# FF2 of a two-block transformer kernel: gate and up as seven block products, and a down phase of its own

## The reference

```python
h = rmsnorm(x, pre_ffn_w[l])
f = (jax.nn.silu(h @ w_gate[l]) * (h @ w_up[l])) @ w_down[l]
x = x + rmsnorm(f, post_ffn_w[l])
```

## Time and profile before

| | us |
|---|---|
| median of 3 runs | 2928.12 |
| lowest, highest run | 2925.88, 2928.41 |
| span of the profiled execution | 2927.6 |

### The profile page before, as it was taken

How to read it: one execution, slowest core, us unless ns; L and a number is a source line. 1 busy time by engine, 2 the same in 40 slices (tenths; PEclk the granted TensorE clock), 3 DMA queues, 4 the chain that set the end, 5 groups by cost and what they waited for, 6 DMA issues and landing times.

```text
span 2927.6 us, 31598 instructions
## 1 busy us (share of the span) xinstructions
PE 2866.2 (98%) x13123; PEld 2327.1 (79%) x13123; DVE 1388.7 (47%) x1658; ACT 961.0 (33%) x1266; POOL 368.1 (13%) x328
## 2 busy tenths in 40 slices
PE   9999999999999999999999999999999999999997
PEld 7877678888888888788878888666787888888886
DVE  6775544453535354543234444665655213233335
ACT  4313442321312121321236656654353221111112
POOL 1213112000000000111002222133321000000003
PEclk9999999999999999999999999999999999999999
DMA  3215523111111111244523331674641111111113
GB/s 117 87 72 140 151 60 108 51 40 55 44 56 40 54 37 61 69 148 159 195 80 101 99 101 59 181 226 146 228 139 69 37 58 40 56 38 62 37 61 126
DMA packets 88623, 270.01 MB, mean 92 GB/s; under 512 B 12568, under 2 KB 17304, under 8 KB 88480
## 3 DMA queue, kind: packets, MB, share of 16 engines
q1 hardware_dynamic: 73984, 221.61, 24.2%
q0 software_dynamic: 14496, 46.38, 4.6%
HBM read 215.35 MB, written 52.59 MB: 92 GB/s over the span
## 4 chain that ended last, share of the span: by engine, by line
PE 84%; DVE 7%; ACT 4%; issue 2%; POOL 1%; DMA 1%; SPq 0%; DVEq 0%; POOLq 0%; ACTq 0%
PE ps L213 83%; DVE cacc L184 1%; ACT PB L178 1%; PE ps L216 1%; POOL ga L181 1%; DVE PB L184 1%; DVE YA L181 1%; POOL YA L181 0%; DVE AL L184 0%; DMA raw<-in_w_win 0%; DMA RBc<-scr_inv 0%; DVE stk L181 0%; DVE sqacc L181 0%; ACT gt L178 0%; DVE cv L181 0%
## 5 line engine op out<-in xcount | busy, mean ns | idle before, releaser
L213 PE MATMUL ps<-AH,wh 128*128 128x512 f32 (+1 forms) x2216 | 880.7, 397 | 23.5 <-DVE T L181 5.7
L213 PE MATMUL ps<-AH,wl 128*128 128x512 f32 (+1 forms) x2216 | 865.7, 391 | 0.0
L213 PE MATMUL ps<-AL,wh 128*128 128x512 f32 (+1 forms) x2216 | 865.4, 391 | 0.0
L181 DVE TENSOR_TENSOR wl<-raw,wh 128x1024 fp32r<-128x1024 f32 (+2 forms) x226 | 268.7, 1189 | 808.5 <-ACT wh L178 808.1
L213 PEld LDWEIGHTS ps<-AH,wh 128*128 128x128 f32 (+1 forms) x2216 | 416.1, 188 | 122.8 <-issue 14.4
L178 ACT ACTIVATE wh<-raw 128x1024 fp32r<-128x1024 f32 (+2 forms) x273 | 251.5, 921 | 766.0 <-PE ps L213 759.3
L213 PEld LDWEIGHTS ps<-AH,wl 128*128 128x128 f32 (+1 forms) x2216 | 415.9, 188 | 90.3
L213 PEld LDWEIGHTS ps<-AL,wh 128*128 128x128 f32 (+1 forms) x2216 | 416.5, 188 | 87.8 <-issue 2.9
L213 PE MATMUL ps<-UH,wh 128*128 128x512 f32 (+1 forms) x840 | 325.2, 387 | 0.0
L213 PE MATMUL ps<-UH,wl 128*128 128x512 f32 (+1 forms) x840 | 325.1, 387 | 0.0
L213 PE MATMUL ps<-UL,wh 128*128 128x512 f32 (+1 forms) x840 | 325.1, 387 | 0.0
(11 more groups left out here) (229 smaller groups left out, 3243.5 us busy)
## 6 DMA issues: line engine op xcount, KB each, us to landing
raw<-in_w_up SPq DMA_DIRECT2D x44, 512.0 KB, 3.4
raw<-in_w_gu SPq DMA_DIRECT2D x44, 512.0 KB, 3.4
raw<-in_w_w2in SPq DMA_DIRECT2D x32, 512.0 KB, 4.3
raw<-in_w_down SPq DMA_DIRECT2D x48, 256.0 KB, 2.6
raw<-in_w_down SPq DMA_DIRECT2D x32, 320.0 KB, 2.8
xin<-in_xT SPq DMA_DIRECT2D x16, 512.0 KB, 8.9
stk<-scr_ka SPq DMA_DIRECT2D x32, 256.0 KB, 8.0
raw<-in_w_w2v SPq DMA_DIRECT2D x16, 512.0 KB, 3.5
```

Source lines behind the costliest of these rows:

```text
L181: return Issued(self, self.e.tensor_tensor(out, a, b, op))
L213: return Issued(self, self.e.matmul(out, l, r, start=start, stop=stop))
```

## The change

**Gate and up.** Blocks 0 to 2 (`PLAIN = 3`) are made as before. For the other 19 (`NQ`) the pair gate/up of a block is one 2x2 block product: weights 2 (gate, up) x 2 (channel tiles 0 to 3, 4 to 7), activations 2 (channel tiles 0 to 3, 4 to 7) x 2 (halves of the tokens). It is made by Strassen's form in Winograd's arrangement: seven products of 4 x 3 = 12 matmuls instead of eight. It needs four sums of activation blocks (T1 to T4, made once by VectorE from the float32 values in `YA`, in the four calls `sums(k)`, then split into `TH`/`TL`) and, per hidden block, four sums of weight blocks (`s_sums`, VectorE) before the split of all seven weight blocks (`high` on ACT, `s_lows` on DVE). The seven results go round the eight banks; VectorE combines them (`gate`, `shared`, `shared_end`, `gate_end`, `value`, `value_end`), after ScalarE has copied the first (`taken`).

**Down.** The gated block (`UU`) is written to a DRAM scratch `s_u` (`spill`). After all 22 blocks a down phase runs in four passes p of 22 steps, w = 0 to 87: passes 0 and 1 for the first half of the tokens, 2 and 3 for the second, each for four of the eight output tiles. One step reads a weight piece of 128x512 (`d_load`, `d_high`, `d_low`; nine buffers) and uses the gated block k = w mod 22 (`u_load`, `u_high`, `u_low`); it is 4 x 3 = 12 matmuls into four banks, and the 22 steps are summed in PSUM. Pass 3 stops after 14 steps (`HELD`); ACT copies that partial sum to SBUF, and the other 8 steps are done in two groups of 256 tokens.

```diff
+PLAIN = 3
+NQ = NFF - PLAIN
+DW = 9
+HELD = 14
...
+    PARTS = [("B11", 0), ("B21", 1), ("T2", 5), ("T1", 4), ("B22", 6), ("T3", 2), ("T4", 3)]
...
     def pe_ff2(self, q):
...
+        def part(n, i):
+            name, b = self.PARTS[i]
+            out = self.s_bank(n, i)
+            q.wait_ge(S.sl, 4 * n + {0: 1, 1: 1, 5: 2, 6: 2, 4: 3, 2: 4, 3: 4}[b])
+            h, l = self.s_high(n, b), self.s_low(n, b)
+            for k in range(4):
+                if name[0] == "T":
+                    q.wait_ge(S.tl3, k + 1)
...
+        for n in range(NQ):
+            for i in range(7):
...
+                elif i == 0:
+                    q.wait_ge(S.ev2, 7 * (n - 1))
+                elif i == 1:
+                    q.wait_ge(S.snp, n)
+                else:
+                    q.wait_ge(S.ev2, 7 * (n - 1) + (1, 2, 3, 4, 6)[i - 2] if n else 0)
+                part(n, i)
...
+        for w in range(88):
+            p, k = w // 22, w % 22
+            q.wait_ge(S.dwl, w + 1)
+            q.wait_ge(S.dul, 22 * (p // 2) + k + 1)
+            if k == 0:
+                q.wait_ge(S.fe, 4 * (p - 1))
+            if w == 66:
+                q.wait_ge(S.fmu, 8)
...
+            if p == 3 and k >= HELD:
+                continue
+            for n in range(4):
+                if w == 0:
+                    q.wait_ge(S.snp, NQ)
+                    q.wait_ge(S.ev2, 7 * NQ - 6 if n < 3 else 7 * NQ)
+                last = k == (HELD - 1 if p == 3 else 21)
+                t = down(w, self.d_bank(p, n), n, every, k == 0, last)
...
+        for g in (1, 2):
+            c = slice(0, 256) if g == 1 else slice(256, 512)
+            q.wait_ge(S.fe, 12 if g == 1 else 16)
+            for n in range(4):
+                for k in range(HELD, 22):
+                    t = down(66 + k, self.d_bank(g + 1, n)[:, c], n, c, k == HELD, k == 21)
...
     def act_ff2(self, q):
...
+        for k in range(2):
+            second(k)
         self.w_high(q, TILE["gu", ("u", 1)])
+        second(2)
+        up(TILE["gu", ("u", 0)], 0)
         self.norm_sqrt(q, 7, 4, 4)
         q.wait_ge(S.nrow, 7)
         q.act(self.RB[:, HALF[1]], self.bank(5), ACT.Copy).then_inc(S.nrb)
...
+        up(TILE["gu", ("u", 0)], 1)
+        sums_high(0)
+        second(3)
+        silu(0)
+        sums_high(1)
+        self.w_high(q, TILE["gu", ("g", 2)])
+        sums_high(2)
+        up_whole(1)
+        silu(1)
+        self.w_high(q, TILE["gu", ("u", 2)])
+        sums_high(3)
+        for b in (0, 5, 4, 2):
+            high(0, b)
...
     def dve_ff2(self, q):
...
+        def s_sums(n):
+            q.wait_ge((S.sg0, S.sg1)[n % 2], 16 * (n // 2 + 1))
+            q.wait_ge((S.su0, S.su1)[n % 2], 16 * (n // 2 + 1))
+            q.wait_ge(S.prd, 7 * (n - 1))
+            a11, a12, a21, a22, s1, s2, s4 = [self.s_raw(n, b) for b in range(7)]
+            q.tt(s1, a21, a22, ALU.add).then_inc(S.ss)
             q.wait_own()
+            q.tt(s2, s1, a11, ALU.subtract).then_inc(S.ss)
+            q.wait_own()
+            q.tt(s4, s2, a12, ALU.subtract).then_inc(S.ss)
+            q.tt(a21, a11, a21, ALU.subtract).then_inc(S.ss)
...
+            if more:
+                s_lows(n + 1, 3)
+            else:
+                for w in range(7):
+                    d_low(w)
+                    if w < 4:
+                        u_low(w)
+            value(n)
+        value_end(NQ - 1)
...
+        for w in range(88):
+            if w >= 7:
+                d_low(w)
...
+            for p in range(3):
+                if w == 22 * (p + 1) + 2:
+                    evacuate(p)
...
+            if 67 <= w < 71:
+                q.wait_ge(S.nrow, 8)
+                for n in (2 * (w - 67), 2 * (w - 67) + 1):
+                    q.wait_ge(S.sD, 8)
+                    q.stt(self.YD[:, n, HALF[0]], self.YD[:, n, HALF[0]], self.V("postff", n), self.bank(6), ALU.mult,
+                          ALU.mult).then_inc(S.fmu)
...
     def sp_ff2(self, q):
...
+        def up_load(n):
+            q.wait_ge(S.prd, 7 * (n - 1))
+            q.dma(self.SWR[n % 2][:, 2:4, :].rearrange("p a b -> p (a b)"),
+                  self.io["w_gu"][("u", PLAIN + n), :, :]).then_inc((S.su0, S.su1)[n % 2], 16)
...
+        q.wait_ge(S.tr3, 16)
...
+        gate_load(0)
+        up_load(0)
```

More of the change, by code:

```diff
@@ L76, in weight_tiles @@
     t += [("w2out", (half, n), 1024) for half in range(2) for n in range(NT)]
[L77 to L81, removed]
+    for i in range(PLAIN):
+        t += [("gu", ("g", i), 1024), ("gu", ("u", i), 1024)]
     return t
@@ L110, in gemm_events @@
             out += [(s, 0), (s, 1)]
-    return out + [(LAST8 + n, g) for g in range(3) for n in range(NT)]
+    return out
 EVENTS = gemm_events()
@@ L400, in __init__ @@
[L400 to L403, removed]
+        self.snap = [Area(nc, lo + at * 1024, lo + at * 1024 + 2048).get("snap", [P, 512]) for at in (4, 6, 112)]
+        self.GG = Area(nc, lo + 8 * 1024, lo + 12 * 1024).get("gg", [P, NTOK])
+        self.UU = Area(nc, lo + 12 * 1024, lo + 16 * 1024).get("uu", [P, NTOK])
@@ L405, in V @@
+        self.DWT, self.DWR = [], []
+        for at in (-24, -20, -16, -12, -8, -4, 76, 8, 12):
+            one = Area(nc, lo + at * 1024, lo + at * 1024 + 4096)
+            self.DWR.append(Area(nc, one.lo + 2048, one.hi).get("dwr", [P, 512])[:, :])
+            self.DWT.append(tuple(one.get("dwt", [P, 512], F32R)[:, :] for _ in range(2)))
     def V(self, name, i=0, p0=0, p1=P):
@@ new lines, in down, with stats @@
+        def down(w, out, n, c, first, last):
+            wh, wl = self.DWT[w % DW]
+            uh, ul = self.DU[w % 22]
+            ws = slice(n * P, n * P + P)
+            q.mm(out, wh[:, ws], uh[:, c], first, False)
+            q.mm(out, wh[:, ws], ul[:, c], False, False)
+            return q.mm(out, wl[:, ws], uh[:, c], False, last)
+        def stats(n, t0, t1, b):
+            for t in range(t0, t1):
+                i = q.mm(self.bank(b)[:, t - t0:t - t0 + 1], self.accD[:, t * P:t * P + P], self.ones[:, 0:1], True, True)
+            i.then_inc(S.nst)
@@ new lines, in dve_ff2 @@
+        self.w_low(q, TILE["gu", ("u", 1)])
+        gate_half(0)
+        self.norm_recip(q, 7, self.rc8[:, 4:8], 4)
+        gate_half(1)
+        sums(0)
+        sums(1)
+        gated(0)
+        self.w_low(q, TILE["gu", ("g", 2)])
+        sums_low(0)
+        sums_low(1)
+        sums(2)
+        gate_whole(1)
+        gated(1)
+        self.w_low(q, TILE["gu", ("u", 2)])
+        sums_low(2)
+        sums(3)
+        sums_low(3)
+        s_sums(0)
+        s_lows(0, 0, 1, 2, 3)
+        gate_whole(2)
@@ new lines, in scaled @@
+        def scaled(n):
+            c = slice(512, 768)
+            q.wait_ge(S.nrow, 9)
+            q.wait_ge(S.sD, 16)
+            q.stt(self.YD[:, n, c], self.YD[:, n, c], self.V("postff", n), self.bank(1)[:, 0:256], ALU.mult,
+                  ALU.mult).then_inc(S.fmu)
+        out(1, 4)
+        for n in range(5, 8):
+            out(1, n)
+            square(1, n - 1)
+        square(1, 7)
+        out(2, 4)
+        out(2, 5)
+        square(2, 4)
+        self.norm_recip(q, 9, self.last_col(1), 2)
@@ L3147, in dve_ff2 @@
+        out(2, 6)
+        square(2, 5)
+        for n in range(4):
+            scaled(n)
+        out(2, 7)
+        square(2, 6)
+        square(2, 7)
+        for n in range(4, 8):
+            scaled(n)
         self.norm_recip(q, 10, self.last_col(2), 2)
-        c = GROUPS[2]
-        scales = self.bank(6)[:, 0:256].unsqueeze(1).to_broadcast([P, 4, 256])
+        c = slice(768, 1024)
+        scales = self.bank(2)[:, 0:256].unsqueeze(1).to_broadcast([P, 4, 256])
         for n in (0, 4):
```

682 lines of the change are left out of this document (427 added, 255 removed), and 4 rows, old and new, of the table SHARED.

## The result

The changed kernel takes 2906.60 us (median of 4 runs, 2905.17 to 2908.76) against 2928.26 for the kernel before (4 runs): a ratio of 0.9928, 95% interval 0.9914 to 0.9943, 21.7 us less. The forecast was 2909.

What follows compares the result with a forecast made beforehand. TensorE, busy 98% of the span, was taken as the bound. Blocks ending at 2627.5 us, plus down steps, seams, statistics and the last 38.0 us, gave a 2908.3 us span, median 2908.8; forecast range 2901 to 2917, overall 2887 to 2923.

Steps and rivals of the forecast that it cites:

- Matmuls and blocks: 19 gate/up blocks: 228 fewer matmuls at 0.2266 us save 51.7 us; each block lasts 19.04 us, with no waits inside.
- Rival D: Inside the blocks: TensorE waits in each for weight low halves or a bank, 2936 to 3018 us; chance 0.07.
- the 4.8 us of cover: Inside each block: VectorE works 14.2 of 19.04 us, leaving 4.8 us spare.
- Way in: Entry to FF2: TensorE waits 3.9 us before gate 2 and 3.3 before block 3; 13.1 us with the clock.
- half clock: Behind TensorE waits of about 3 us or more: clock falls to 1.2 GHz, costing 2.9 us on top.
- First seam: Blocks to down, step 0: 3.2 us wait for the last block's value plus 2.0 for the clock, 5.2 us.
- Second seam: Step 66: TensorE waits 7.5 us for VectorE's scalings of the first half; 10.4 us with the clock.
- Third seam: Step 80: 4.8 us wait for weight pieces split behind ScalarE's copies of held banks; 7.7 us with the clock.
- Statistics and end: From the first 256-column matmul to the span's end: 42.0 us less 5.4 plus 1.4, so 38.0 us.
- The five places: TensorE idle before gate 2 (3.9), block 3 (3.3), in step 0 (3.2), before steps 66 (7.5) and 80 (4.8).
- Rival B: At the seams: they are cheaper or the clock holds, 2898 us, or 2893 with the entry wait halved; chance 0.18.
- C: Matmuls slower with other operands, or seams at their upper bounds: 2915 to 2924 us, 2929 with both; chance 0.17.

Runs made afterwards that it cites:

- e7: Changed kernel plus three extra 128x1024 VectorE instructions in each of the 19 blocks, behind the value: 2910.86 us.
- e8: Changed kernel plus six extra 128x1024 VectorE instructions in each of the 19 blocks, behind the value: 2958.92 us.
- e9: Changed kernel with gate 2's and up 2's weights split ahead of the activation sums, VectorE's sums run together and wide low halves last: 2897.82 us.
- e3: Changed kernel with seven of the last block's nine down-phase low halves on VectorE moved behind that block's value: 2904.25 us.
- e1: Changed kernel with VectorE's eight scalings of the first half put three weight pieces earlier, ahead of pass 2's results: 2899.37 us.
- e6: Changed kernel with 32 TensorE matmuls of 128x512, whose result nobody reads, ahead of the wait of step 66: 2901.74 us.
- e5: Changed kernel with the three re-orderings e1, e2 and e3 together: 2887.03 us.
- e10: Changed kernel with the edits of e5 and e9 together: 2874.72 us.
- e4: Changed kernel with only gate 2's weight split (ScalarE) and low half (VectorE) put ahead of the activation sums: 2907.17 us.
- e2: Changed kernel with ScalarE's copies of the four held banks put behind its last weight piece (87): 2903.74 us.

## Why the prediction was right

**Matmuls and blocks.** 51.7 us from 228 x 0.2266: the count is exact, the pitch too (19 us a block). VectorE was costed at 14.2 us per block; it takes 13.4. Rival D stays out: VectorE can take on 3.7 us more per block without a wait (e7) and 7.3 not (e8), and the 4.8 us of cover in the prediction, 5.6 by the rows, lie between.

**Way in, 13.1 us.** The waits are 3.87 and 4.10, for 3.9 and 3.3. Block 3's was longer since the load of up took 5.6 us for 5.0; the four sums took 2.8 as counted. ScalarE's 128x2048 took 1.92 for 1.9. The half clock cost 2.8 us behind gate 2 (24.33 us from the first to the last of 96 starts, for 95 x 0.2266 = 21.53) for 2.9, but only 1.65 behind block 3, again for 2.9. So a wait 0.8 us too small and a half clock 1.2 us too large nearly cancel. e9 took 11.4 away and left 1.1: 12.5.

**First seam, 5.2 us.** Wait 3.17 for 3.2; e3: 5.05 in all, so 1.9 for the clock. I had taken 2.0 for it, between nothing and 2.9, without a row; that it fits is luck.

**Second seam, 10.4 us.** Wait 7.70 for 7.5; e1: 10.8, e6: 2.8 of it the clock. GpSimd's part was 1.7 us by the changed kernel's rows. I had 9.0 us for the seam if each low half waited for a full GpSimd instruction of 1.38 us. The two low halves began 0.43 and 0.15 us into one of 1.26 us, waited for its end and lost 0.7 and 1.0 us. The rule of the Trainium skill (SBUF — State Buffer, "Who interferes with whom"), that the two exclude each other, agrees with these rows; what failed was my working from it, which is its upper bound. The earlier trace rows already show the same: the instruction of 1.78 us ended at 2195.81, 0.54 us behind the GpSimd one beside it.

**Third seam, 7.7 us.** Wait 5.14 for 4.8 (the prediction's terms add to 4.7). The clock behind it costs 28.41 - 26.59 = 1.8 us (256-column matmuls up to the last statistics, changed kernel against e5), for 2.9: 6.9.

**Statistics and end.** I had 38.0 us from the first 256-column matmul to the end, with the clock counted at the seam; e5, where the clock stays up behind step 80, has 2887.2 - 2849.19 = 38.0. One reading was wrong and did no harm: the prediction calls the 1.56 us wait TensorE's only late one, but the trace before has others in the statistics, the longest 2.03 us ahead of the last sums at 2917.14.

**The step that was mis-sized** is the constant 2.9 us of half clock, taken from one wait. It was 2.8 at its largest and 1.4 at its smallest behind one and the same wait of 7.7 us, 1.65 behind block 3 and 1.8 at step 80. The five places come to 12.5 + 5.1 + 10.8 + 6.9 = 35.3 us in place of 36.4.

**The sum.** FF2 is 19.9 us shorter, for 2927.6 - 2908.3 = 19.3 forecast. The span missed by more (2902.9 for 2908.3), and 4.8 us of that lie ahead of the wait for `AL`, in code that didn't change: 2207.58 against 2202.74. The median, 2906.6 for 2908.8, fits better than the span, and that is luck: the prediction put the median 0.5 us above the span, as it had been for the kernel before, but here the profiled run was the fastest of the four, its own time 2905.17 lies 2.3 above its span, and the median lies 3.7 above. Rival B's 2898 and C's bounds did not come. B's figure for all seams gone was 2872.7, 55.4 us less; e10's median is 2874.7. By FF2 time it is 50.7 us less, and its waits of 1.11 and 1.89 us and the 1.45 us of half clock behind the second are 4.5 of the 4.7 that are missing.

## What to carry to other kernels

When a bound engine gets less work, add up its waits at the entry, the seams and the end of the changed part: here 35 of some 55 us went back there, while the steady state behaved as computed. Find for each the queue order that makes it, and move together whatever feeds the next wait: mending the first of two in a chain (e4) only moved it, mending the chain (e9) gave 11 us. Compare inside a trace, from an event ahead of the change, when runs differ by as much as an edit.

## What was not expected of the hardware

The clock's fall did not go by the length of the wait alone, so "about 3 us or more" in the prediction was no limit. At step 80 it fell behind 1.96 (e2) and 1.89 us (e10) and stayed up behind 1.74 (e5). In e7 it fell, ahead of FF2, behind a wait of 1.24 us at 2086.09, and behind the same wait in the changed kernel (2086.50) it stayed up. In e8 the same 2.15 us wait stands ahead of the blocks at 2403.55 and 2425.03; behind the first the clock stayed up, behind the second it fell for a while:

```profile
2405.00:2407.00 2.00, 2.00 (x10) 1.65 (x9) 1.86 (x4) 0.00 (x0) 0.00 (x0) 1.00 0.00 0
2426.00:2428.00 2.00, 2.00 (x7) 1.52 (x6) 1.90 (x3) 0.00 (x0) 0.00 (x0) 0.50 0.00 0
```

Of the nine blocks that start between 2403.55 and 2575.36 it fell so in three, and each still lasted 21.48 us, since VectorE paced them: where TensorE isn't the bound, half clock costs nothing. What decides the fall, the runs leave open. Matmuls whose result nobody reads held the clock up (e6) and cost nothing that the trace shows.

VectorE and GpSimd, both reading two operands from SBUF, took turns by whole instructions (the rows under e1). A low half that began second ended 0.55 us after the GpSimd instruction, so what it lost depended on when it began, here 0.7 and 1.0 us.
